# Two-block network: root mean squares applied to results, operands split before normalisation

## The reference, cut to what matters

```python
def rmsnorm(x, g):
    x32 = x.astype(jnp.float32)
    y = x32 * lax.rsqrt(jnp.mean(x32 * x32, axis=-1, keepdims=True) + EPS)
    return y.astype(x.dtype) * g
# block 1, layer: h = rmsnorm(x, norm_g); proj = h @ w_in, split into 15 parts
#   (conv gates, short conv, window attention, neighbourhood attention dq dk dv dz); x += y @ w_out
# between the blocks: x = rmsnorm(x, final_norm_g)
# block 2, layer: h = rms_norm(x, g_mix[l]); proj = h @ w_in[l]
#   u_pool, q_lat, kv_lat, u_lru, gate_logit; two latent RMS norms (q: 384, kv: 256 features);
#   gates = sigmoid(gate_logit + b_gate); merged = sum of gates * branches; x += merged @ w_out
#   h = rms_norm(x, g_ffn[l]); x += square(relu(h @ w_ff1)) @ w_ff2
# at the end: rms_norm(x, g_final)
```

## Time and profile before

| | us |
|---|---|
| median of 3 runs (2278.48 to 2278.99) | 2278.51 |
| the profiled execution | 2277.89 |
| its span in the profile | 2275.8 |
| PE busy | 2069.6 |
| DVE busy | 1297.8 |
| POOL busy | 1067.6 |
| ACT busy | 751.4 |

### The profile page before, as it was taken

How to read it: one execution, slowest core, us unless ns; L and a number is a source line. 1 busy time by engine, 2 the same in 40 slices (tenths; PEclk the granted TensorE clock), 3 DMA queues, 4 the chain that set the end, 5 groups by cost and what they waited for, 6 DMA issues and landing times.

```text
span 2275.8 us, 30810 instructions
## 1 busy us (share of the span) xinstructions
PE 2069.6 (91%) x9660; PEld 1717.5 (75%) x9660; DVE 1297.8 (57%) x2241; ACT 751.4 (33%) x1101; POOL 1067.6 (47%) x1301
## 2 busy tenths in 40 slices
PE   5998887998887899979999999979998999999997
PEld 4877666876665788868788888867787788888886
DVE  5377776377768755464545535465556445445445
ACT  2332332332332344442232232234444323232231
POOL 3333244334233344456556655634435455656653
PEclk9999898999887899989999999989999999999998
DMA  4112112212111111222222222211122222222221
GB/s 154 64 55 74 38 56 81 75 55 74 38 56 66 56 69 62 74 93 92 93 93 93 92 92 102 102 62 60 71 74 76 91 93 93 93 93 92 100 96 62
DMA packets 28052, 179.53 MB, mean 79 GB/s; under 512 B 4000, under 2 KB 4128, under 8 KB 7456
## 3 DMA queue, kind: packets, MB, share of 16 engines
q1 hardware_dynamic: 24192, 169.88, 20.8%
q10 hardware_dynamic: 3744, 8.21, 1.1%
HBM read 175.98 MB, written 2.10 MB: 78 GB/s over the span
## 4 chain that ended last, share of the span: by engine, by line
issue 47%; POOL 35%; PE 17%; DVE 0%; POOLq 0%; DVEq 0%; ACT 0%
POOL W_lo L422 35%; PE bank L436 16%; POOLq L417 0%; DVE X L1647 0%; PE bank L486 0%; PE bank L479 0%; POOLq L419 0%; POOL spare L413 0%; DVE TMP L1300 0%; DVE PR L1345 0%; DVE PRE L1342 0%; DVE X L2009 0%; DVE PR L2006 0%; DVEq L182 0%; POOLq L422 0%
## 5 line engine op out<-in xcount | busy, mean ns | idle before, releaser
L422 POOL TENSOR_TENSOR W_lo<-W_raw,W_hi 128x256 fp32r<-128x256 f32 x1280 | 1065.6, 868 | 1176.3 <-ACT W_hi L885 1176.2
L436 PE MATMUL bank<-H_hi,W_hi 128*128 128x512 f32 x1392 | 563.1, 404 | 21.9 <-POOL W_lo L422 19.1
L436 PE MATMUL bank<-H_lo,W_hi 128*128 128x512 f32 x1392 | 551.8, 396 | 0.0
L436 PE MATMUL bank<-H_hi,W_lo 128*128 128x512 f32 x1392 | 551.6, 396 | 0.0
L885 ACT ACTIVATE W_hi<-W_raw 128x2048 fp32r<-128x2048 f32 x161 | 307.5, 1910 | 395.3 <-PE bank L436 382.6
L436 PE MATMUL bank<-Y_hi,W_hi 128*128 128x512 f32 x836 | 338.3, 405 | 22.7 <-DVE Y_lo L1285 12.7
L436 PE MATMUL bank<-Y_lo,W_hi 128*128 128x512 f32 x836 | 335.0, 401 | 0.0
L436 PE MATMUL bank<-Y_hi,W_lo 128*128 128x512 f32 x836 | 333.8, 399 | 0.0
L436 PEld LDWEIGHTS bank<-H_hi,W_hi 128*128 128x128 f32 x1392 | 268.7, 193 | 84.2 <-issue 24.0
L436 PEld LDWEIGHTS bank<-H_hi,W_lo 128*128 128x128 f32 x1392 | 267.2, 192 | 58.4
L436 PEld LDWEIGHTS bank<-H_lo,W_hi 128*128 128x128 f32 x1392 | 268.6, 193 | 53.5
(11 more groups left out here) (265 smaller groups left out, 2708.6 us busy)
## 6 DMA issues: line engine op xcount, KB each, us to landing
W_raw<-in_stream SPq DMA_DIRECT2D x160, 1024.0 KB, 4.8
BT<-in_bias ACTq DMA_DIRECT2D x8, 448.0 KB, 3.5
X<-in_x ACTq DMA_DIRECT2D x4, 512.0 KB, 10.2
out<-X SPq DMA_DIRECT2D x8, 256.0 KB, 2.2
BT<-in_rope ACTq DMA_DIRECT2D x2, 512.0 KB, 3.4
MC<-in_causal ACTq DMA_DIRECT2D x2, 256.0 KB, 2.9
MS<-in_window ACTq DMA_DIRECT2D x1, 320.0 KB, 11.1
CS<-in_rope ACTq DMA_DIRECT2D x1, 256.0 KB, 2.6
```

Of the source, the lines that this page charges most:

```text
L422: ins = nc.gpsimd.tensor_tensor(W[1][:, s, part], W_raw[:, s, part], W[0][:, s, part].bitcast(F32), ALU.subtract)
L436: mm = pe.matmul(out, lhs[a], rhs[b], start=(not begun and k == 0 and a == 0 and b == 0), stop=(not more and k == n - 1 and a == 1), skip_ ...
```

## The change

In block 1 the order of the first units becomes dq, dk, dz, dv. Two pairs of buffers swap roles from layer to layer: RAW holds the split of X * gain (later the branch results), NORMED the split of X * gain * factor. dq and dk read RAW, and VectorE multiplies their results with the spread factor (dq into CA, dk into PRE; dk writes the banks TB); all other units read NORMED, and dz is a second by-tiles unit. The sums run after dq in the first layer and inside its by-tiles unit in the second, the spread after dk0. The RAW split for the next layer is made behind each addition to X in the o phase (`norm_lo` on VectorE, the high part straight from X on ScalarE).

Between the blocks the final gain is folded into block 2's first gain (GX), X itself is normalised later, in two groups of four products (`norm_between`) among the latents, and two sums with one root give both factors.

In block 2 everything reads the split of X * gain. The factor (RB2) is multiplied onto results: the gates (`gate`, into GT, tanh then in place), the third gates (`third_gate`, into PR), the received pool and recurrent tiles, and kr; the latent norms take it up in a scaled epsilon. f3 makes the next layer's split. The mean for each of these roots is now a VectorE operation of its own (`mean`). The loops over layers are unrolled; the inner loops stay.

```diff
-B1_UNITS = ["dq", "dk", "dv", "dz", "av", "au", "bc", "bx", "cq", "ck", "cz", "bb", "bz", "az",
+B1_UNITS = ["dq", "dk", "dz", "dv", "av", "au", "bc", "bx", "cq", "ck", "cz", "bb", "bz", "az",
...
+    RB1 = TMP[:, 1, :]
...
+    def operands(l):
+
+        return (H, Y) if l % 2 == 0 else (Y, H)
...
-        with pe.Fori(0, DEPTH) as l:
-            pe_norm(pe, b1, l, "n", ACC1)
+        for l in range(DEPTH):
+            RAW, NORMED = operands(l)
...
+                out = (TB if name[:2] == "dk" else G)[c]
...
-            for mm in by_tiles(pe, 0, H, lambda kt: pe.wait_ge(b1.lo.sem, b1.lo.at(l, f"n{kt}"))):
+            for mm in by_tiles(pe, 0, RAW, lambda kt: pe.wait_ge(b1.lo.sem, b1.lo.at(l, f"n{kt}")),
+                               {6: lambda: pe_sums(pe, b1, l, "n", (ACC1,))} if l else {}):
                 mm.then_inc(b1.done.sem, 1)
-            for name in ("dk0", "dk1", "dv0", "dv1"):
-                chunk(name)
+            if not l:
+                pe_sums(pe, b1, l, "n", (ACC1,))
+            chunk("dk0")
+            pe_spread(pe, b1, l, "n")
+            chunk("dk1")
+            begin_unit(1, l, 2)
+            for c in range(2):
+                free_bank(4 + c)
+            for mm in by_tiles(pe, 0, NORMED, lambda kt: pe.wait_ge(b1.lo.sem, b1.lo.at(l, f"m{kt}"))):
+                mm.then_inc(b1.done.sem, 1)
+            chunk("dv0")
             scores(0)
-            chunk("dz0")
-            chunk("dz1")
+            chunk("dv1")
...
-        pe_sums(pe, bf, 0, "n", ACC1, (b1.acc, DEPTH))
-        pe_spread(pe, bf, 0, "n", bank=OB)
-
-
-        with pe.Fori(0, DEPTH) as l:
-            pe_norm(pe, b2, l, "n", ACC2)
-
+        for l in range(DEPTH):
             begin_unit(2, l, 0)
-            pe.wait_ge(b2.free.sem, b2.free.at(l, "kv0") - 1)
-            for mm in by_tiles(pe, 0, H, lambda kt: pe.wait_ge(b2.lo.sem, b2.lo.at(l, f"n{kt}"))):
+            if l:
+                pe.wait_ge(b2.free.sem, b2.free.at(l, "kv0") - 1)
+            else:
+                pe.wait_ge(b1.free.sem, b1.free.at(DEPTH - 1, "o31"))
+            for mm in by_tiles(pe, 0, H, lambda kt: pe.wait_ge(b2.lo.sem, b2.lo.at(l, f"n{kt}")),
...
                 if name == "q00":
-                    pe_sums(pe, b2, l, "kv", ACC2)
+                    pe_spread(pe, b2, l, "n", bank=OB)
+                    if not l:
+                        pe_spread(pe, bf, 0, "between", TMP[:, 1, :], TB[0])
+                    pe_sums(pe, b2, l, "kv", (ACC2,))
...
+        act.wait_ge(gains_in, 16)
+        for k in range(KT):
+            if k % 2 == 0:
+                act.wait_ge(x_in[k // 2], 16)
+            hi(b1, 0, f"n{k}", H[0][:, k, :], X[:, k, :], scale=PARF[:, k:k + 1])
+        load_b1(0)
...
             begin("dq0")
+            root(b1, l, "n")
+            begin("dk0")
             for k in range(KT):
-                act.wait_ge(b1.pre.sem, b1.pre.at(l, f"n{k}"))
-                hi(b1, l, f"n{k}", H[0][:, k, :], PRE[:, k % 2, :])
-            for name in ("dq0", "dq1", "dk0", "dk1", "dv0", "dv1"):
-                chunk(name, begun=name == "dq0")
+                act.wait_ge(b1.pre.sem, b1.pre.at(l, f"m{k}"))
+                hi(b1, l, f"m{k}", NORMED[0][:, k, :], PRE[:, k % 2, :])
+            begin("dz0")
+            for name in ("dq0", "dq1", "dk0", "dk1"):
+                chunk(name, begun=True)
+            for name in ("dz0", "dz1", "dv0"):
+                chunk(name, begun=name == "dz0")
...
+                name = f"o{k // 2}{k % 2}"
+                if k in (2, 4, 6):
+                    begin(name)
+                act.wait_ge(b1.free.sem, b1.free.at(l, name))
+                if l + 1 < DEPTH:
+                    col = GAINS["b1"][l + 1] + k
+                    hi(b1, l + 1, f"n{k}", NORMED[0][:, k, :], X[:, k, :], scale=PARF[:, col:col + 1])
+                else:
+                    hi(b2, 0, f"n{k}", H[0][:, k, :], X[:, k, :], scale=GX[:, k:k + 1])
...
+        def norm_lo(b, l, k, gain, to=H):
+
+            dve.wait_ge(b.hi.sem, b.hi.at(l, f"n{k}"))
+            dve.wait_ge(*own.last(1))
+            nc.vector.scalar_tensor_tensor(to[1][:, k, :], X[:, k, :], gain, to[0][:, k, :].bitcast(F32),
+                                           ALU.mult, ALU.subtract).then_inc(b.lo.sem, own.event(b.lo, l, f"n{k}"))
...
+            for c in range(2):
+                dve.wait_ge(b1.done.sem, b1.done.at(l, f"dq{c}"))
+                dve.wait_ge(*own.last(c))
+                nc.vector.tensor_tensor(CA[:, c, :], G[c][:, :], RB1, ALU.mult) \
+                    .then_inc(b1.free.sem, own.event(b1.free, l, f"dq{c}"))
+            for k in range(KT + 1):
+                if k < KT:
+                    col = GAINS["b1"][l] + k
+                    dve.wait_ge(*own.last(0))
+                    nc.vector.scalar_tensor_tensor(PRE[:, k % 2, :], X[:, k, :], PARF[:, col:col + 1], NB[:, :],
+                                                   ALU.mult, ALU.mult) \
+                        .then_inc(b1.pre.sem, own.event(b1.pre, l, f"m{k}"))
+                if k:
+                    lo(b1, l, f"m{k - 1}", NORMED[1][:, k - 1, :], PRE[:, (k - 1) % 2, :], NORMED[0][:, k - 1, :])
+            for name in ("dq0", "dq1", "dk0", "dk1", "dz0", "dz1"):
                 chunk(name)
             softmax_max(0)
...
+        def norm_between(ks):
+
+            for k in ks:
+                col = GAINS["between"] + k
+                dve.wait_ge(*own.last(1))
+                nc.vector.scalar_tensor_tensor(X[:, k, :], X[:, k, :], PARF[:, col:col + 1], TB[0][:, :],
+                                               ALU.mult, ALU.mult).then_inc(dve_step, own.step())
...
+            dve.wait_ge(b2.bc.sem, b2.bc.at(l, "n"))
+            dve.wait_ge(*own.last(1))
+            nc.vector.tensor_copy(RB2[:, :], OB[:, :]).then_inc(dve_step, own.step())
...
+                    def gate(s):
+                        g, c = divmod(s, 2)
+                        out = GT[:, bass.ds(4 * j + (g * 8 + 2 * jj + c), 1), :].rearrange("p a n -> p (a n)")
+                        dve.wait_ge(b2.done.sem, b2.done.at(l, f"g{jj}{s}", "h", j))
+                        dve.wait_ge(*own.last(1))
+                        nc.vector.tensor_tensor(out, G[c][:, :], RB2[:, :], ALU.mult) \
+                            .then_inc(b2.free.sem, own.event(b2.free, l, f"g{jj}{s}", "h", j))
...
+            def third_gate(seg, i, c):
+
+                dve.wait_ge(b2.done.sem, b2.done.at(l, f"t{c}", seg, i))
+                dve.wait_ge(*own.last(1))
+                nc.vector.tensor_tensor(PR[:, c, :], G[c][:, :], RB2[:, :], ALU.mult) \
+                    .then_inc(b2.free.sem, own.event(b2.free, l, f"t{c}", seg, i))
...
+            third_gate("mid", 0, 0)
...
+                        ins.then_inc(dve_step, own.step())
+                        continue
+                    ins.then_inc(b2.pre.sem, own.event(b2.pre, l, f"x{n}", seg))
+                    squares(ACC2, X[:, n, :], n == 0, (b2.acc, l + 1) if n == KT - 1 else None)
+                    if l + 1 < DEPTH:
+                        col = GAINS["b2"][l + 1] + n
+                        norm_lo(b2, l + 1, n, PARF[:, col:col + 1])
```

More of the change, by code:

```diff
@@ L60 @@
 NP2 = _n
+GAINS = {"b1": (0, KT), "b2": (2 * KT, 3 * KT), "between": 4 * KT, "last": 5 * KT}
 COUNTS = []
@@ L153, in b1_splits @@
 def b1_splits():
-    out = [f"n{k}" for k in range(KT)] + ["dq0", "dq1", "dk0", "dk1", "dv0", "dv1"]
+    out = [f"n{k}" for k in range(KT)] + [f"m{k}" for k in range(KT)] + ["dq0", "dq1", "dk0", "dk1", "dv0", "dv1"]
     for i in range(2 * STEPS):
@@ L165, in b1_splits, with filled @@
     return out
+def filled(name):
+    return [i for i, n in FILL.items() if n == name][0]
 def head_names(jj):
@@ L314, in _build @@
     bf = Block()
-    bf.ss, bf.rt, bf.dg, bf.bc = (Count(sem(f"norm_{n}F"), 0, [("", 1, ["n"])])
-                                  for n in ("sum", "root", "diag", "spread"))
+    bf.ss, bf.ms, bf.rt = (Count(sem(f"norm_{n}F"), 0, [("", 1, ["n"])]) for n in ("sum", "mean", "root"))
+    bf.dg, bf.bc = (Count(sem(f"norm_{n}F"), 0, [("", 1, ["between", "n"])]) for n in ("diag", "spread"))
     final = Count(sem("final"), 0, [("", 1, [str(k) for k in range(KT)])])
@@ L1266, in _ @@
             own.leave(3)
-            down(60, 0, "f3", 0)
-            act.wait_ge(*own.last(1))
-            nc.scalar.activation(spare_a[:, :], ones[:, 0:1], ACT.Copy).then_inc(act_step, own.step())
-        own.leave(DEPTH)
-        root(bf, 1, "n", D)
+            for k in range(KT):
+                if k in (2, 4, 6) and l + 1 < DEPTH:
+                    prep(2, l, 60 + k // 2 - 1, (b2.done, l, f"d{k - 1}", "f3", 0))
+                elif k in (2, 4):
+                    prep(2, l, 60 + k // 2 - 1, (b2.done, l, f"d{k - 1}", "f3", 0))
+                if l + 1 < DEPTH:
+                    act.wait_ge(b2.pre.sem, b2.pre.at(l, f"x{k}", "f3"))
+                    col = GAINS["b2"][l + 1] + k
```

(26 more changed lines are left out.)

377 lines of the change are left out of this document (209 added, 168 removed).

## The result

| | before | changed |
|---|---|---|
| median, us | 2278.03 (7 runs) | 2284.4 (2283.18 to 2289.58, 7 runs) |
| span of the profiled execution | 2275.8 | 2280.8 |
| PE busy | 2069.6 | 2099.6 |
| mean granted TensorE clock | 0.946 | 0.934 |

The changed kernel takes 1.0036 times as long as the one before, 95% interval 1.0027 to 1.0046: slower by 0.36%, where 1% faster was forecast. The median lies 16 us above the upper end of the range. PE's idle time did fall, from 206 to 181 us; but PE was busy 30 us longer with the same 9660 matmuls. So the loss is not in the waits themselves, it is in the rate at which PE works.

The account below looks back on a forecast made before the run. PE, busy 2069.6 of 2275.8 us, bounds the kernel; only its idle time and slower clock can shrink. -5.5 + 7.5 + 15.2 + 7.65 - 0.5 - 1.7 - 0.3 = 22.4 us gain, median 2256, range 2245 to 2268.

Parts of the forecast that it names:

- First layer: Block 1, first layer: later Y_hi and a new 8 us wait before dv0 lose 5.5 us, bounds -3 to -9.
- Second layer of block 1: PE goes on right after the last o, with a new wait before dv0: +7.5 us, bounds +3 to +16.
- Entry and second layer of block 2: Sums, spreads and diagonals leave PE's path: +15.2 us at the entry, +7.65 in the second layer.
- rival 3: Covers hold: no wait before dv0, norm_between in idle time; gain 42 us, 2236 us; chance 0.09 (below 2247).
- Gates: Block 2: gate multiplies -0.5 us, first third gate delaying W_lo in the middle -1.7, mean before the last norm -0.3.
- Rival 1: Each of 48 gate multiplies lands on PE's path, 33 us: 2289 us; chance 0.06 in full.
- Rival 2: Wait before dv0 is 12 us in both block-1 layers; gain only 12 us, 2266 us; chance 0.15.
- Rival 4: PE still meets the sums first, only loop unrolling gains: 2275 us at best; chance 0.07 shared with half of rival 1.

Follow-up runs that it names:

- fill_wait: Changed kernel with 32 unused 512-column matmuls in place of PE's wait before dv0, both block-1 layers: 2237.75 us, 0.9837 of the kernel before.
- fill_after: Changed kernel with 16 unused 512-column matmuls between the wait and dv0, the wait kept: 2250.44 us, 0.9892 of the kernel before.
- dv_banks: Changed kernel with dv0 and dv1 written to banks OB and NB instead of G: 2283.02 us, 1.0024 of the kernel before.
- dv_early: Changed kernel with dv0 and dv1 in banks OB and NB and ACT's copy of dv's unit behind the fourth high part: 2228.04 us, ratio 0.9787.
- gates_twice: dv_early with every multiply of a gate by the RMS factor made twice on DVE: 2231.71 us, 0.98 of the kernel before.
- before_wait: Kernel before with ACT's copy of dv's unit made seven times, so PE waits before dv0 in both block-1 layers: 2335.2 us, ratio 1.0265.
- before_wait_short: Kernel before with ACT's copy of dv's unit made four times, for a shorter wait before dv0: two runs, 2304.6 and 2324.3 us, ratio 1.0163.

## Why the prediction was wrong, step by step

**First layer: the step that failed.** The prediction had the new wait, its place, its releaser and nearly its length (8 us; it is 7.26, behind ZB). It failed at the price of what stands behind the wait, in the words "PE idles 8 us and is slow afterwards (1.6 us more). Two dv chunks of 10.8". The prediction shows no row for the 1.6; it is the loss of 512-column matmuls behind a wait (7.37 us and not 5.72 for the 24 behind the wait of 2.25 us at 184.26 in the kernel before; 13.3 us and not 10.9 for the by-tiles unit of the earlier trace rows). The 10.8 came from dv chunks that PE had entered at the full clock. Behind this wait come 192 matmuls of 128 columns. dv0, scores and dv1 last 44.2 us and not 23.3, and the transposes and the next chunk take another 2.6: 23.5 us in the first layer and 23.8 in the second. Some 2 us are won back later, and at the end the traces of the changed kernel and of fill_wait are 45 us apart. No row of the kernel before showed a dv chunk behind a wait; the term should have been bounded from above by its whole length at the other clock level, 10.8 more for each chunk. At that price the sum itself, 22.4 us of gain, is a loss of 17.6 (an estimate: 22.4 - 2 x (21.6 - 1.6)).

The rest of the step was right, as the ACT and DVE rows of the chain show, which answer to the earlier trace rows:

```profile
53.76 1.90 ACT L913 ACTIVATE W_hi<-W_raw 128x2048 fp32r<-128x2048 f32 x1
...
61.95 1.28 ACT L1017 ACT_TABLE_LOAD   x1
63.25 0.60 ACT L1017 ACTIVATE TMP<-bank 128x512 f32<-128x512 f32 x1
...
63.94 0.69 DVE L1567 SCALAR_TENSOR_TENSOR ZB<-TMP,bank 128x512 f32<-128x512 f32 x1 [0.77 <-ACT TMP L1017]
```

From the last Y_hi (53.86) to ZB (64.63) it is 10.8 us; 11.3 was the sum (its parts, as they are listed, give 11.4 before the overlap of 0.3, and not 11.6). The chain itself began 5 us earlier than forecast: the spread starts at 40.13 and lasts 0.8 us, at the full clock, where it was put behind 43.5 with 2.0 us at the lower one, and the first unit's copy ended at 9.4 and not at 11.1. Without the clock the first layer would have gained 1.1, not lost 5.5. The table load takes 1.28, the tanh starts 1.30 after it began, and the load itself starts 0.02 behind the end of the high part in front of it. The Trainium skill, "ScalarE: Activation LUTs", "What ACT_TABLE_LOAD costs", adds a drain to the load; the trace of the changed kernel shows none, neither ahead of the load nor behind it.

**Second layer of block 1.** PE went on 0.83 us after the last o, dv0 began 42.8 us after it (43.9 forecast), and dv0 to dv1 took 20.9 longer than at the full clock: the stretch lost 10.7, and gains 10.2 with the clock held, against the +7.5 of the sum.

**Entry and second layer of block 2.** Right in mechanism, both terms too small by 3 us: +18.3 and +10.5. At the entry spread "kv" came 30.8 us after the last o (32.6 in the sum; the softplus chain took 5.5 us, not 6.5) and the stretch to spread "q" was 21.0, not 22.3. Of norm_between the first four products run beside the spread. The other four stand in DVE's work without a pause before or behind them, and PE waits for what follows:

```profile
773.01 2.71 DVE L1767 SCALAR_TENSOR_TENSOR X<-X,PARF,bank 128x512 f32<-128x512 f32 x4
...
779.75 1.50 PE L496 MATMUL bank<-ones,PR 128*128 128x1 f32 x8 [2.74 <-DVE SPARES L1359]
```

By this reading about half of norm_between is on the path, and rival 3, which has it in idle time, is right for the other half only; that the wait would go with these four products was not tried.

**Gates.** -0.5 and -1.7 and -0.3 were forecast; the two long stretches of block 2 lost 1.1 and 2.0 (2.5 in fill_wait). The -1.7 did not come where it was expected: in the middle PE's longest wait behind W_lo is 7.19 us (7.28 before), and the next one, now behind a third gate's tanh (ACT PR), 5.00 (4.79 before, behind W_lo). About 3.5 us of the later stretch's loss is one place: DVE stands 4.14 us, released by nothing that the profile shows, at a turn of the heads' loop, and PE's wait for K_lo there is 6.42 us, against 2.4 to 2.9 at the other turns:

```profile
1647.39 0.68 DVE L1913 TENSOR_TENSOR PRE<-bank,GT 64x512 f32<-64x512 f32 x1 [4.14 <-issue]
```

It stands at the same turn in every trace of the changed kernel with single multiplies (fill_wait, fill_after, dv_banks and dv_early too, 4.1 to 4.4 us), and at no other turn; in gates_twice it is missing. The DMA view of 1643.2 to 1647.9 has three packets on the queue that it calls "instruction"; dv_early has the same three around its stand, and gates_twice none at this turn. So the loading of instructions is a candidate, but no experiment tried it.

**The rivals.** Rival 1 falls by gates_twice. Rival 2 named the right place, but the wait was 7.26 us and not 12 (and its gain of 12 does not follow from its own words: 4 us more of wait in each of two layers leaves 14.4 of the 22.4). Rival 4 falls by the timelines. Rival 3 is close to what dv_early shows, 2228 us against its 2236, with no wait in front of dv0. Nearly every sign that the prediction named came true (the wait and its releaser, the by-tiles unit 0.83 us behind the last o, the entry in 51.8 us); none of them asked for the clock.

The sum of 22.4 holds twice 1.6 us for the clock, so it is 25.6 without this term; the spans of the kernel before and of fill_wait are 40 us apart (38 by the medians beside each other). So the other terms together were too small, and the one term that was priced at 1.6 us a layer cost over 22. Only because the others erred to the good side is the kernel 6 us slower and not some 20; that is luck.

## What to carry to other kernels

Where a change puts a wait in front of a stretch, price the stretch behind it from a row in which the same kind of matmul came behind a wait, and where there is none, bound it by its whole length at the lower clock: here waits of 2 to 8 us cost their own length and some 19 to 24 us more, because 192 matmuls of 128 columns followed, while in front of 512-column work a wait cost its own length and some 2 us. Two remedies worked in this kernel: to fill the wait (fill_wait), and to give the chunk that the edit moved banks and weights that are ready when PE comes to it (dv_early). Sixteen 512-column matmuls between the wait and the narrow ones gave back 34 us (fill_after). A forecast that takes a duration from a row must also take the clock of that row.

## What was not expected of the hardware

- In these traces the 128-column matmuls of dv (each with its own weight load) kept the clock at the level that they found once it had settled: 1.00 through 192 of them behind 512-column matmuls without a gap (fill_wait, fill_after, dv_early), 0.50 to 0.53 through 192 of them behind a wait (changed kernel, before_wait, dv_banks). The six 512-column matmuls on 64 partitions between the chunks, 2.9 us, did not raise it; the sixteen on 128 partitions of fill_after did, but their window's 0.71 over 5.2 us means that they too began with about 3 us at 0.50 (an estimate). So whether the partitions matter is open.
  The Trainium skill, "TensorE: Matmul & The Clock Gate", "What you observe", shows 64 back-to-back bf16 matmuls of 128 columns that come to the full rate, where they start about 56 ns apart. The split fp32 ones of dv start 0.112 us apart at the full clock and 0.214 at the lower one, and did not come to the full rate in 41 us (before_wait): for this chunk the measurement differs, and it decides. Whether the type, the spacing or the weight loads between them are the reason was not tried.
- The fall can come after the wait: with 2.07 us of waiting the first twelve matmuls of dv0 ran at full rate, then the clock dropped (before_wait_short). The kernel before has it too: behind the wait of 2.25 us at 184.26 the first three matmuls of 512 columns start 0.23 to 0.33 us apart and the next eight some 0.43.
- 32 matmuls without any use in each layer of block 1 made the changed kernel 2.0% faster (2237.75 against 2284.4).
